# Order of work at eight waits of TensorE in a two-block transformer kernel

## What is computed

```python
# first block: eight heads with a top-k search (a), eight dilated heads (b)
rel = einsum('bqhd,bsd->bqhs', q_idx, k_idx)
score = einsum('bqhs,bqh->bqs', relu(rel), w_idx) * idx_scale
top_val, top_idx = lax.top_k(score, 128)              # the "search": rounds of 8 values
...
x = x + einsum('bse,ed->bsd', mixed, w_out)
# second block: selected and window branches, softmax, weighted by gates
o = g[0] * o_cmp + g[1] * o_sel + g[2] * o_win
...
h = rms_norm_2(x, norm_mlp)                           # "h3" below
x = x + square(relu(h @ w_ff1)) @ w_ff2
```

## Time and profile before

| | |
|---|---|
| three timed runs | 1015.06, 1015.14, 1015.5 us; median 1015.14 |
| profiled execution | 1015.04 us, span 1013.2 us, mean granted TensorE clock 0.999 |
| busy | TensorE 999.0, VectorE 704.0, ScalarE 567.3, GpSimd 443.4 us |
| 170 to 290 us, the first attention | TensorE busy 116.86 of 120 us |
| 520 to 600 us, most of the second attention | TensorE busy 78.54, VectorE 61.25, ScalarE 64.15, GpSimd 39.91 of 80 us |

### The profile page before, as it was taken

How to read it: one execution, slowest core, us unless ns; L and a number is a source line. 1 busy time by engine, 2 the same in 40 slices (tenths; PEclk the granted TensorE clock), 3 DMA queues, 4 the chain that set the end, 5 groups by cost and what they waited for, 6 DMA issues and landing times.

```text
span 1013.2 us, 14351 instructions
## 1 busy us (share of the span) xinstructions
PE 999.0 (99%) x5134; PEld 821.2 (81%) x5134; DVE 704.0 (69%) x1235; ACT 567.3 (56%) x1034; POOL 443.4 (44%) x435
## 2 busy tenths in 40 slices
PE   9999999999999999999999999999999999999997
PEld 7788878778778898888887788888888888888886
DVE  5578898788985356824567789994232325999997
ACT  8455444777872355545577884644344346554565
POOL 0023012666737302900155430008679875774563
PEclk9999999999999999999999999999999999999999
DMA  9533321336254784233200328548999952443552
GB/s 340 106 99 94 104 63 43 84 76 191 68 216 170 238 275 136 55 83 84 61 3 1 99 91 273 183 169 293 337 355 342 358 180 65 155 144 137 207 188 83
DMA packets 109543, 158.31 MB, mean 156 GB/s; under 512 B 7024, under 2 KB 69232, under 8 KB 109472
## 3 DMA queue, kind: packets, MB, share of 16 engines
q1 hardware_dynamic: 96176, 142.81, 43.2%
q10 hardware_dynamic: 12768, 12.88, 4.0%
q0 software_dynamic: 528, 1.70, 1.0%
HBM read 131.55 MB, written 25.82 MB: 155 GB/s over the span
## 4 chain that ended last, share of the span: by engine, by line
PE 88%; DVE 6%; ACT 2%; issue 1%; DMA 1%; SPq 1%; POOL 0%; ACTq 0%; DVEq 0%
PE bank L1084 59%; PE bank L1626 5%; PE bank L1627 5%; PE bank L1628 5%; PE bank L1479 2%; PE bank L1266 2%; PE bank L1488 2%; PE bank L1237 2%; PE bank L1502 2%; DVE x L2483 1%; PE bank L1250 1%; DMA arena<-in_rel_bias 1%; DVE stats L2482 1%; DVE u_lo L2360 1%; PE bank L1389 1%
## 5 line engine op out<-in xcount | busy, mean ns | idle before, releaser
L2972 DVE TENSOR_TENSOR w_lo<-wring,w_hi 128x1024 fp32r<-128x1024 f32 x32 | 50.4, 1576 | 107.4 <-ACT w_hi L2203 107.2
L2360 DVE TENSOR_TENSOR u_lo<-wring,u_hi 128x1024 fp32r<-128x1024 f32 (+2 forms) x69 | 83.3, 1215 | 53.2 <-ACT u_hi L1803 52.7
L1084 PE MATMUL bank<-u_hi,h_hi 128*128 128x512 f32 (+1 forms) x288 | 110.9, 385 | 0.1
L1084 PE MATMUL bank<-u_hi,h_lo 128*128 128x512 f32 (+1 forms) x288 | 109.3, 379 | 0.0
L1084 PE MATMUL bank<-u_lo,h_hi 128*128 128x512 f32 (+1 forms) x288 | 109.0, 378 | 0.0
L1803 ACT ACTIVATE u_hi<-wring 128x1024 fp32r<-128x1024 f32 (+2 forms) x66 | 66.6, 1009 | 71.0 <-PE bank L1084 54.1
L1084 PE MATMUL bank<-h_hi,w_hi 128*128 128x512 f32 (+1 forms) x272 | 102.7, 378 | 0.9 <-DVE h_lo L2401 0.9
L1084 PE MATMUL bank<-h_hi,w_lo 128*128 128x512 f32 (+1 forms) x272 | 102.3, 376 | 0.0
L1084 PE MATMUL bank<-h_lo,w_hi 128*128 128x512 f32 (+1 forms) x272 | 102.1, 377 | 0.0
L1084 PE MATMUL bank<-h_hi,u_hi 128*128 128x512 f32 x224 | 93.5, 417 | 0.4 <-ACT arena L1742 0.2
L1084 PE MATMUL bank<-h_hi,u_lo 128*128 128x512 f32 x224 | 88.2, 394 | 0.0
(11 more groups left out here) (447 smaller groups left out, 2648.8 us busy)
## 6 DMA issues: line engine op xcount, KB each, us to landing
wring<-in_w_in SPq DMA_DIRECT2D x60, 512.0 KB, 3.9
wring<-in_w_ff ACTq DMA_DIRECT2D x12, 1024.0 KB, 8.6
wring<-sums_kept SPq DMA_DIRECT2D x16, 768.0 KB, 4.2
wring<-in_w_ff SPq DMA_DIRECT2D x22, 512.0 KB, 6.5
wring<-in_w_ff SPq DMA_DIRECT2D x32, 256.0 KB, 3.4
sums_kept<-wring SPq DMA_DIRECT2D x22, 256.0 KB, 5.0
arena<-in_w_out SPq DMA_DIRECT2D x16, 256.0 KB, 3.9
sets_kept<-arena SPq DMA_DIRECT2D x8, 512.0 KB, 4.4
```

Of the source, the lines that this page charges most:

```text
L1084: last = mm(b, lhs, rhs, start=(start and n == 0), stop=(stop and n == 2))
L2360: done = v.tensor_tensor(u_lo[raw_place(u)][:, cols], raw_unit(u)[:, cols], u_hi[hi_place(u)][:, cols].bitcast(F32), ALU.subtract)
L2972: v.tensor_tensor(cut(w_lo[ring3(m)]), src, cut(w_hi[ring3(m)]).bitcast(F32), ALU.subtract).then_inc(w_lo_done, 1)
```

## The change

Six edits of order, and no operation added or taken away.

1. `WO_HIGH`: ScalarE's copy of output weight piece 2 moves from pass 48 (entry 49) to pass 50 (entry 51), and with it VectorE's subtraction of that piece by one pass.
2. `value1` of the first half goes between the two heads' transposes in passes 8, 16, 24 and 32.
3. The last two position tiles of feed-forward tile 0 start with the terms that need only the high halves, each half with a wait of its own; the terms that need the low part come behind.
4. `per_slot["qa"]`: one search round moves from the second slot to the third.
5. `collect2` of groups 0 to 5: half 0 moves to VectorE's pass 8o+18, half 1 to pass 8o+20, each behind the scores and ahead of the low parts. Before, both were at the end of pass 8o+16. Groups 6 and 7 stay.
6. In passes 4, 8, ... 28 the reciprocal goes ahead of the first score.

```diff
-    WO_HIGH = {46: 0, 47: 1, 49: 2, 53: 3, 54: 4, 57: 5, 58: 6, 64: 7}
+    WO_HIGH = {46: 0, 47: 1, 51: 2, 53: 3, 54: 4, 57: 5, 58: 6, 64: 7}
...
                 if 4 <= t < NS + 4:
                     turn1(t - 4)
+                    if ahead:
+                        value1(t // NH - 1, 0, 0)
                     turn1(t - 3)
                 if t >= 8 and t % NH == 0:
-                    value1(t // NH - 1, 0, 0)
+                    if not ahead:
+                        value1(t // NH - 1, 0, 0)
                     value1(t // NH - 1, 0, 1)
...
-            pe.wait_ge(h_lo_done, halves("h3", NT - 1, 1) + 1)
             for c in range(2):
-                ff_tile(c, 2 * P, S).then_inc(a_full, 1)
+                pe.wait_ge(h_hi_done, halves("h3", NT - 1, c) + 1)
+                ff_tile(0, 2 * P, S, range(4 * c, 4 * c + 4), (0, 2) if c == 0 else (0,))
+            pe.wait_ge(h_lo_done, halves("h3", NT - 1, 1) + 1)
+            ff_tile(0, 2 * P, S, range(KC), (1,))
+            ff_tile(0, 2 * P, S, range(4, KC), (2,)).then_inc(a_full, 1)
+            ff_tile(1, 2 * P, S).then_inc(a_full, 1)
...
-            per_slot = {"qb": (1, 2, 2, 2), "vb": (3, 3, 3, 3), "ka": (3, 4, 3, 2), "qa": (3, 3, 2, 1), "va": (2, 2, 2, 2)}
+            per_slot = {"qb": (1, 2, 2, 2), "vb": (3, 3, 3, 3), "ka": (3, 4, 3, 2), "qa": (3, 2, 3, 1), "va": (2, 2, 2, 2)}
...
-            def collect2(o):
+            def collect2(o, sides=range(2)):
                 i, g = o // G2, o % G2
-                dve.wait_ge(lo_rows_done, GROUPS + o + 1)
-                if o >= 1:
-                    dve.wait_ge(attn_done, o)
+                if 0 in sides:
+                    dve.wait_ge(lo_rows_done, GROUPS + o + 1)
+                    if o >= 1:
+                        dve.wait_ge(attn_done, o)
...
-                for r in range(2):
+                for r in sides:
...
             for t in range(0, NS + 10, 2):
-                if t < NS:
+                late_scores = 0 < t < NS and steps2[t][0] <= 1 and t % 4 == 0
+                if t < NS and not late_scores:
                     score2(t)
                 if 2 <= t < NS + 2:
                     dve.wait_ge(e_done, NS + t)
                     v.reciprocal(den2[:, t - 2:t], den2[:, t - 2:t]).then_inc(rden_done, 1)
+                if late_scores:
+                    score2(t)
                 if t < NS:
                     score2(t + 1)
+                if 18 <= t < NS and t % NH in (2, 4):
+                    collect2((t - 18) // NH, (t % NH // 2 - 1,))
                 if 4 <= t < NS + 4:
                     prob_low(t - 4)
                     prob_low(t - 3)
-                if t >= 16 and t % NH == 0:
+                if t >= NS and t % NH == 0:
                     collect2((t - 16) // NH)
```

More of the change, by code:

```diff
@@ L1609, in _ @@
             ff_tile(1, 0, 2 * P, range(6, KC))
+            for c in range(2):
+                pe.wait_ge(h_hi_done, halves("h3", NT - 1, c) + 1)
+                ff_tile(0, 2 * P, S, range(4 * c, 4 * c + 4), (0, 2) if c == 0 else (0,))
             pe.wait_ge(h_lo_done, halves("h3", NT - 1, 1) + 1)
-            for c in range(2):
-                ff_tile(c, 2 * P, S).then_inc(a_full, 1)
+            ff_tile(0, 2 * P, S, range(KC), (1,))
+            ff_tile(0, 2 * P, S, range(4, KC), (2,)).then_inc(a_full, 1)
+            ff_tile(1, 2 * P, S).then_inc(a_full, 1)
             pe.wait_ge(r_free, out2_added(NT - 1))
```

## The result

The changed kernel takes 1033.74 us in the median (1031.43 to 1038.2, six runs) against 1014.8 for the kernel before; the ratio of the two sets of runs, by their means, is 1.0195, with a 95% interval of 1.0179 to 1.0212. It is slower, as forecast, but by 19 to 20 us and not by the 14.3 of the sum. 1029.3 was forecast. The median lies just inside the upper end of the range, 1034.0; the time by the ratio, 1.0195 x 1014.8 = 1034.6, lies just outside. The executions also scatter. The six runs of the kernel before stay within 1.1 us, those of the changed one spread over 6.8.

A forecast was written before the change was run, and what follows sets the result against it. TensorE's own stream, busy 999.0 of 1013.2 us, was taken to bound the kernel. The terms 16.2 - 0.9 - 0.5 - 0.5 = 14.3 us, on top of 1015.04, gave 1029.3 us; range 1021.5 to 1034.

The forecast's parts named there:

- The block: Second attention, groups 0 to 5: GpSimd's late addition holds up the scaling that TensorE's transposes need; 16.2 us lost.
- The second head's share: Second attention: the second head's scaling also comes late, adding 0.33 us in five groups; in group 1 the next wait absorbs it.
- group 5: Last of the six delayed groups in the second attention: transposes 3.68 us late, taken as 3.3 because scores come sooner.
- The clock: TensorE's granted clock, 1.00 from 520 to 600 us before the change, should stay 1.00.
- (b): Rival: TensorE's clock falls in the longer waits of the second attention, costing 7.4 us in all, 1036.7 us; chance 0.08.
- (a): The forecast itself: GpSimd's queue block in the second attention costs its full amount, 1023.5 to 1033 us; chance 0.78.
- The tail: Feed-forward tail: products put ahead outlast TensorE's 0.86 us wait for the last low half; 0.9 us gained.
- The first attention: Value products fill a wait for GpSimd's scaling, 0.5 us gained; moved weight piece lets a low part come sooner, 0.5 gained.
- The search round: Projection stage: the wait at line 1142 goes, but TensorE then waits for a bank at 149.79; 0 gained.
- (c): Rival: the block is shorter because later waits absorb part, 6 to 9 us in all, 1019 to 1022.5 us; chance 0.05.
- (d): Rival: no block in the second attention and the edits do what they say, 1011.2 us; chance 0.06.
- (e): Rival: over the whole kernel, gains and losses lie within 2 us of each other; chance 0.03.

The follow-up runs named there:

- add_behind: Changed kernel, but GpSimd's addition of groups 0 to 5 stands behind the scaling of head 8o+17, not ahead of that of head 8o+16; 1015.88 us.
- add_late: Changed kernel, but GpSimd's addition of groups 0 to 5 stands behind the scaling of head 8o+19; 1013.09 us.
- filled: Changed kernel with 112 extra identity transposes by TensorE, placed ahead of its waits in the six groups; 1031.47 us.
- round_later: no_split with one search round moved from the last slot of group qa to the first of group va, behind the sum of squares; 1011.64 us.
- no_split: Changed kernel with the collecting sums put back into pass 8o+16, both halves together, all other edits kept; 1013.05 us.
- split_short: Kernel before with the collecting sums split in groups 2 and 3 alone; 1020.64 us.
- split_long: Kernel before with the collecting sums split in groups 0, 4 and 5 alone; 1028.6 us.
- split_only: Kernel before with only the collecting sums of groups 0 to 5 split over passes 8o+18 and 8o+20; 1034.76 us.

## Why the prediction was right on the cause and short on the time

- **The block.** Right in place and mechanism, shown by `add_behind` and `add_late`. Twelve waits totalling 14 to 16 us were named; the list shows six, of 14.6 us. The second head's share is in the rows all the same: the four transposes of group 0 take 0.97 us where they took 0.60 before, 0.37 more, against 0.33 forecast. GpSimd's additions stood idle for 5.6 to 7.0 us and not 4 to 6. In size the term was 16.2 and measured 17.1 net, in which up to 0.1 us a group is the fillers' own. Two steps were too low. For group 5, 3.3 was forecast; the wait is 3.8 us, of which the 0.5 us at line 1479 that went away is to be taken off, and to which some 0.16 us are to be added, because the idle time is counted from the modelled end of the last product. In group 1 the next wait was to absorb the second head's 0.33; it only went from 0.33 in the kernel before to 0.17 in `filled`. These two make some 0.3 of the 0.9 us, and 0.04 more per second head, if group 0 stands for all, another 0.2. The term's bound, 19, holds it.
- **The clock: the step that failed.** "The granted clock should stay 1.00" is wrong: the sum has no term for it, and this is what put the time at the edge of the range. The forecast's own numbers had waits of about 3 us, longer than any in the kernel before; so (b) was no alternative to (a) but a term on top of it, and 0.08 was far too little. The runs showed four falls in the profiled execution, 4.5 us within the six groups, and 2.3 us between the median and `filled`. Priced at 7.4 us it was too high for the median (2.3 us above `filled`) and about right for the slowest execution (1038.2, which is 6.7 above it). Half of the kernel's first 4.93 us is 2.5 per fall, for three falls; one fall measured 1.5, four together 4.5, and they came behind waits of 2.0 us too, not behind the three longest alone. The mean granted clock of the six executions is not the same either: 0.996 at 1031.43 us and 0.987 and 0.988 at 1038.2. The Trainium skill (TensorE: Matmul & The Clock Gate, Part 1) says that the place of the clock's rise at a kernel's start varies between runs of one kernel; the falls vary here as well. `filled` shows that the falls go when the idle time is filled; the waits that no fall followed show that the length of a wait alone doesn't decide.
- **The tail** (-0.9) measured about -1.1, within what can be told. **The first attention** (-0.5 and -0.5) measured about -1.1 for the two together; their shares weren't measured apart, but the waits in the list fell as said, and the one of 208.96 stayed, with 0.5 us, now ahead of the value products. **The search round** (0) was right, for the reason given, and `round_later` shows it: with the sum of squares one round earlier the wait goes, and 1.4 us with it (the median against that of `no_split`, from other sets of runs).
- **The sum.** Without the clock, the terms gave 1029.3. `no_split` plus the measured block is 1013.05 + 17.1 = 1030.2, so 0.9 us of the miss lie in the block and the rest, 3.6 us of 1033.74 and up to 8 in the slowest execution, in the clock. Counted against `filled`, which also pays the wait at 626.33, the clock is 2.3 us of the median and 2.2 were missing without it.
- **Rivals (c), (d), (e)** fell. The condition of (d), an addition that doesn't hold up the queue, was met only in `add_late`, and even there its time, 1011.2, wasn't: 1013.09 was measured, since the 0.9 of line 1479 went from the list but not from the time, and the 1.0 of the search round didn't come. In (c), 9 us less 1.9 gives 1022.1 and not 1022.5; nothing hangs on it.

## What to carry to other kernels

When an instruction is moved later on one engine, look up who waits for it in another engine's in-order queue, and what stands behind that waiter. Move the waiter along by the same distance: here one changed condition in GpSimd's loop was worth 20 us. When a forecast itself makes the bounding engine stand idle, its clock is a term of the sum, not a rival to it.

## What the runs showed that was not expected

How long TensorE waits doesn't say by itself whether its clock falls. Waits of 1.57 us (`split_short`) and 2.00 us (group 1 after) were followed by a fall, waits of 1.61 us (`split_short`) and 3.05 us (`split_long`) were not; in `split_only` the same 3.05 and 1.62 us were. Three executions of the changed kernel took 1031 to 1033 us, two 1038.2, with the same instructions.

A fall needs no change in the attention. Two later executions of the kernel before took 1017.76 and 1018.38 us, at a mean granted clock of 0.996 and 0.997, where the others took 1014.25 to 1015.88 at 0.998 to 1.0; there is no profile of these two. In the profiled execution of `add_late`, which took 1016.63 us where the other ten took 1012.5 to 1014.1, TensorE waited twice at the start, once for a transfer, and ran its next products 0.43 us apart:

```profile
23.98 1.03 PE L1176 MATMUL bank<-arena 32*16 32x512 f32 x2 [0.89 <-DMA arena<-in_rel_bias]
...
26.11 1.55 PE L1183 MATMUL bank<-arena 128*128 128x128 f32 x8 [0.89 <-DVE arena L2445]
...
28.32 0.63 PE L1084 MATMUL bank<-u_lo,h_hi 128*128 128x512 f32 x1
28.75 0.63 PE L1084 MATMUL bank<-u_hi,h_hi 128*128 128x512 f32 x1
```
